# The head of a two-block decoder program: input in two transfers, identity and columns on the weights' queue, the root table loaded first, squares in one pass a row

## The reference, cut to what matters

```
def rmsnorm(x, g):                       # x: 256 x 1024
    y = x * rsqrt(mean(x * x, axis=-1) + EPS)
    return y * g

for i in range(2):                       # first block, two layers
    h = rmsnorm(x, norm1_g[i])
    z = h @ w_in[i] + b_in[i]            # q, k, v, gates ... of two mixers
    ...                                  # mixers, merge, feed-forward, gate
x = rmsnorm(x, final_g)
...                                      # second block, on x
```

## Time and profile before

| | |
|---|---|
| median of three runs | 3247.7 us |
| the profiled execution, its own time | 3248.43 us |
| its span, first to last instruction | 3246.6 us |
| around the span | 1.8 us |
| PE busy | 3170.3 us, 98% |
| DVE, ACT, POOL busy | 65%, 46%, 15% |
| mean granted clock of TensorE | 0.991 |

### The profile page before, as it was taken

The page is one execution under the profiler, slowest core; times in us unless marked ns, Lnnn a source line. Parts: engine busy times, 40 slices in busy tenths (PEclk is TensorE's granted clock), DMA queues, the critical chain, the costliest instruction groups (busy, mean ns, idle before and its releaser), DMA issues.

```text
span 3246.6 us, 49505 instructions
## 1 busy us (share of the span) xinstructions
PE 3170.3 (98%) x20652; PEld 2800.4 (86%) x20652; DVE 2109.0 (65%) x3115; ACT 1499.2 (46%) x1717; POOL 494.2 (15%) x278
## 2 busy tenths in 40 slices
PE   8999999999999999989999999999999999999998
PEld 8797889797978897878999989888769999999887
DVE  6775665577766656685967755555677867655555
ACT  6444454573444545612544444444344454444443
POOL 0000000000000000010766600000003766200000
PEclk9999999999999999999999999999999999999999
DMA  6454645444546554303454475555424544665553
GB/s 228 153 190 167 220 179 186 168 157 168 187 162 219 182 195 171 144 28 112 177 183 153 142 255 201 195 195 194 169 91 156 182 163 150 220 220 193 192 192 125
DMA packets 87656, 565.12 MB, mean 174 GB/s; under 512 B 10192, under 2 KB 10208, under 8 KB 23568
## 3 DMA queue, kind: packets, MB, share of 16 engines
q1 hardware_dynamic: 80496, 534.81, 45.9%
q0 software_dynamic: 6944, 27.21, 2.5%
HBM read 552.54 MB, written 9.44 MB: 173 GB/s over the span
## 4 chain that ended last, share of the span: by engine, by line
PE 53%; DVE 5%; ACT 1%; issue 1%; DVEq 0%; ACTq 0%
PE bank L2099 22%; PE bank L2127 7%; PE bank L2131 7%; PE bank L2126 7%; PE bank L2080 4%; ACT w_hi L2257 1%; PE bank L1797 0%; PE bank L1792 0%; PE bank L1793 0%; PE bank L2064 0%; DVE w_lo L2534 0%; DVE ymix L2755 0%; PE bank L1827 0%; PE bank L1828 0%; PE bank L1831 0%
## 5 line engine op out<-in xcount | busy, mean ns | idle before, releaser
L2257 ACT ACTIVATE w_hi<-raw 128x2048 fp32r<-128x2048 f32 x291 | 558.0, 1918 | 717.0 <-PE bank L2131 377.0
L2534 DVE TENSOR_TENSOR w_lo<-raw,w_hi 128x2048 fp32r<-128x2048 f32 x222 | 510.1, 2298 | 540.7 <-ACT w_hi L2257 539.9
L1055 DVE TENSOR_TENSOR w_lo<-raw,w_hi 128x2048 fp32r<-128x2048 f32 x200 | 458.1, 2292 | 319.3 <-ACT w_hi L816 317.5
L816 ACT ACTIVATE w_hi<-raw 128x2048 fp32r<-128x2048 f32 x201 | 384.9, 1917 | 443.7 <-PE bank L546 239.5
L2099 PE MATMUL bank<-act_hi,w_hi 128*128 128x256 f32 x2048 | 486.6, 281 | 0.0
L2099 PE MATMUL bank<-act_lo,w_hi 128*128 128x256 f32 x2048 | 482.1, 279 | 0.0
L2127 PE MATMUL bank<-w_hi,c_lo 128*128 128x512 f32 x1024 | 398.7, 389 | 0.0
L2126 PE MATMUL bank<-w_hi,c_hi 128*128 128x512 f32 x1024 | 398.7, 389 | 0.0
L2099 PEld LDWEIGHTS bank<-act_hi,w_hi 128*128 128x128 f32 x2048 | 385.5, 188 | 0.2
L2099 PEld LDWEIGHTS bank<-act_lo,w_hi 128*128 128x128 f32 x2048 | 385.4, 188 | 0.0
L1694 POOL TENSOR_TENSOR w_lo<-raw,w_hi 128x2048 fp32r<-128x2048 f32 x70 | 322.9, 4618 | 329.0 <-ACT w_hi L2257 171.4
(11 more groups left out here) (544 smaller groups left out, 5184.4 us busy)
## 6 DMA issues: line engine op xcount, KB each, us to landing
raw<-weights SPq DMA_DIRECT2D x492, 1024.0 KB, 4.8
row<-rows POOLq DMA_DIRECT2D x48, 256.0 KB, 4.3
spill<-staged SPq DMA_DIRECT2D x32, 256.0 KB, 3.1
hid<-spill SPq DMA_DIRECT2D x32, 256.0 KB, 4.8
y<-w_pe POOLq DMA_DIRECT2D x2, 1024.0 KB, 5.1
ln_row_mix<-ln_rows POOLq DMA_DIRECT2D x4, 512.0 KB, 4.9
hid<-keys POOLq DMA_DIRECT2D x2, 1024.0 KB, 6.3
ln_row_ffn<-ln_rows POOLq DMA_DIRECT2D x4, 512.0 KB, 7.7
```

The lines of the kernel that those rows point to most:

```text
L816: nc.scalar.activation(w_hi[:, k % SPLIT, :], raw[:, k % RAW, :], ACT.Copy).then_inc(hi_ready, 1)
L1055: nc.vector.tensor_tensor(w_lo[:, k % SPLIT, :], raw[:, k % RAW, :], w_hi[:, k % SPLIT, :].bitcast(F32), ALU.subtract).then_inc(lo_ready, 1)
L2257: A.activation(hi_of(k), raw[:, k % RAW, :], ACT.Copy).then_inc(hi_ready, 1)
L2534: V.tensor_tensor(lo_of(k), raw[:, k % RAW, :], hi_of(k).bitcast(F32), ALU.subtract).then_inc(lo_ready, 1)
```

## The change

x comes in two transfers, one a token half, each with a semaphore of its own; the identity goes between them and the columns behind them, both on SP's queue and both ahead of the weights. POOL's queue starts with the gate bias. A new `first_mean_square` loads the table of the root before it waits for x, and then makes for each half one pass of squares over all 1024 columns and the root. `gw_hi` on ACT goes behind the eight `act_hi`, `gw_lo` on DVE behind the eight `act_lo`, in both layers.

```
-    x_loaded = sem("x_loaded")
+    x_loaded = [sem(f"x_loaded{t}") for t in range(TT)]
+    col_first = sem("col_first")
...
-            sp.dma_start(x[:, :, :], x_in).then_inc(x_loaded, 16)
+            sp.dma_start(x[:, 0, :], x_in[:, 0, :]).then_inc(x_loaded[0], 16)
+            sp.dma_start(ident, identity).then_inc(ident_loaded, 16)
+            sp.dma_start(x[:, 1, :], x_in[:, 1, :]).then_inc(x_loaded[1], 16)
+            sp.dma_start(col[:, :], cols[0]).then_inc(col_first, 16)
...
-            pool.dma_start(ident, identity).then_inc(ident_loaded, 16)
...
-                pool.dma_start(col[:, :], cols[layer]).then_inc(col_loaded, 16)
+                    pool.dma_start(col[:, :], cols[layer]).then_inc(col_loaded, 16)
...
+            def first_mean_square():
+
+                act.wait_ge(eps_ready, 1)
+                do(nc.scalar.activation(spare[:, :], eps, ACT.Sqrt))
+                for t in range(TT):
+                    act.wait_ge(x_loaded[t], 16)
+                    do(nc.scalar.activation(junk[:, :], x[:, t, :], ACT.Square, accum_out=ssq[:, t:t + 1]))
+                    do(nc.scalar.activation(rstd[:, t:t + 1], ssq[:, t:t + 1], ACT.Sqrt, bias=eps, scale=1.0 / D), std_ready)
...
-                    if i or layer == 0:
+                    if i:
                         mean_square(3 * layer + i)
-                    if i == 0 and layer == 0:
+                    elif layer == 0:
+                        first_mean_square()
                         split_hi(0, 0, free=False)
                     if i == 0:
-                        act.wait_ge(col_loaded, layer * 32 + 32)
-                        do(nc.scalar.activation(gw_hi ..., ACT.Copy), gw_split)
+                        act.wait_ge(col_first, 16)
+                        if layer:
+                            act.wait_ge(col_loaded, layer * 32 + 16)
...                                      # the eight act_hi
+                    if i == 0:
+                        do(nc.scalar.activation(gw_hi ..., ACT.Copy), gw_split)
...                                      # on DVE: waits for the columns, the eight act_lo, then gw_lo
```

More of the change, by code:

```diff
@@ L820, in front_squares @@
             def front_squares(n):
[L822 to L826, removed]
+                act.wait_ge(front_added, n)
                 for t in range(TT):
@@ L831, in rest_squares @@
             def rest_squares(n, t):
-                if n:
-                    act.wait_ge(half_added, TT * (n - 1) + t + 1)
+                act.wait_ge(half_added, TT * (n - 1) + t + 1)
                 do(nc.scalar.activation(junk[:, CW:D], x[:, t, CW:D], ACT.Square, accum_out=ssq[:, t:t + 1]))
@@ L859, in norm @@
                 def norm(i):
-                    if i or layer == 0:
+                    if i:
                         mean_square(3 * layer + i)
-                    if i == 0 and layer == 0:
+                    elif layer == 0:
+                        first_mean_square()
                         split_hi(0, 0, free=False)
                     if i == 0:
-                        act.wait_ge(col_loaded, layer * 32 + 32)
-                        do(nc.scalar.activation(gw_hi[:, :, :].rearrange("p k n -> p (k n)"), col[:, COL["gatew"]:COL["gatew"] + 64], ACT.Copy), gw_split)
+                        act.wait_ge(col_first, 16)
+                        if layer:
+                            act.wait_ge(col_loaded, layer * 32 + 16)
                     g0 = COL[f"norm{i + 1}"]
@@ L875, in norm @@
                             do(ins, n_hi)
+                    if i == 0:
+                        do(nc.scalar.activation(gw_hi[:, :, :].rearrange("p k n -> p (k n)"), col[:, COL["gatew"]:COL["gatew"] + 64], ACT.Copy), gw_split)
                 def mixed(first, k0, banks=range(KD // 2)):
@@ L1090, in norm @@
                         split_lo(base, 0)
[L1091 to L1095, removed]
+                        dve.wait_ge(col_first, 16)
+                        dve.wait_ge(col_loaded, layer * 32 + 16)
                     g0 = COL[f"norm{i + 1}"]
@@ L1101, in norm @@
                                                   op0=ALU.mult, op1=ALU.subtract), n_lo)
+                    if i == 0:
+                        dve.wait_ge(gw_split, 1 + layer * A_LAYER["gw_split"])
+                        V.tensor_tensor(gw_lo[:, :, :].rearrange("p k n -> p (k n)"), col[:, COL["gatew"]:COL["gatew"] + 64],
+                                        gw_hi[:, :, :].rearrange("p k n -> p (k n)").bitcast(F32), ALU.subtract).then_inc(gw_split, 1)
                 def mixed(first, k0, banks=range(KD // 2)):
```

## The result

| | before | after |
|---|---|---|
| median, 20 runs each (lowest to highest) | 3246.86 us (3240.89 to 3252.16) | 3252.1 us (3244.38 to 3259.97) |
| profiled execution | 3248.43 us | 3253.41 us |
| its span | 3246.6 us | 3251.6 us |
| mean granted clock | 0.991 | 0.991 |

The ratio is 1.0015, 95% interval 1.0009 to 1.0022: 5.2 us slower, with an interval of 2.9 to 7.1. The forecast was 3250.0, 2.3 us slower than the 3247.7 of the three runs shown, and 3252.1 lies just inside its range of 3242.0 to 3252.5. It is slower, as forecast, by twice the forecast step.

The account below looks back on a forecast made before the run. PE bounds the kernel, busy 3170 of 3246.6 us, so only its idle head could be given back. Later first matmul 0.5, cold clock 1.6 and layer 1 0.2 make 2.3 us slower: 3250.0 us, range 3242.0 to 3252.5.

Parts of the forecast that it names:

- Part 1: Head: x's halves land at 4.1 and 5.9, transposes begin at 6.8; this alone gains 5.8 us.
- Part 2: Weight tile 0, sharing the engines with POOL's earlier constants, lands at 13.6 (bounds 8.6 to 14.2), and ACT waits for it.
- Part 3: PE's first real matmul at 16.4, 0.5 us later than before; bounds 4.5 gained to 1.1 lost.
- Part 4: PE idles between transposes and first matmuls, which then run on the low clock: 1.6 us lost, bounds 0 to 3.4.
- The gate product: Rival: the shifted head shortens, lengthens or moves the slow-clock stretch at the gate matmuls; 1.7 us either way, no separate chance.
- Part 5: Layer 1: gw_hi ahead of a copy without slack costs PE some 0.2 us, bounds 0 to 0.25.
- the class: Whole kernel's step against 6.5 us, what the measurement can tell: same 0.91, faster 0.06, slower 0.03.
- half of the gain: Rival: tile 0 lands as before, first matmul 2.4 us earlier, PE gap of 3 us; 3245.5 us, chance 0.22.

Follow-up runs that it names:

- e7: The changed kernel with 5 and 6 unused matmuls behind the halves' transposes, keeping PE busy; median 3264.94 us against 3255.24 for the kernel before.
- e8: The changed kernel with identity and columns back at the front of POOL's queue, x still in halves; 3256.03 us against 3255.24 for the kernel before.
- e2: The kernel before with the new queues alone, ACT waiting for both halves of x and keeping its old list; 3253.42 us against 3247.95.
- e3: The changed kernel with POOL's constants and rows held until weight tile 0 lands, gate bias still first; 3247.78 us against 3247.95 for the kernel before.
- e5: The changed kernel with POOL's gate bias, constants and rows all held until weight tile 0 lands; 3256.2 us against 3255.24 for the kernel before.
- e6: The kernel before with ACT's new order, and POOL's bias, constants and rows held until weight tile 0 lands; 3253.78 us against 3255.24.

## Why the prediction was right, and where its size was off

**Part 1, x by halves.** The first half was forecast to land at 4.1, with bounds of 4.1 and 5.7, and landed at 4.75; first transpose 7.5 against 6.8. The second half was forecast at 5.9 and landed at 11.7. This step failed. The bias was expected on the engines from 5.3, on the end of x or on tile 0; its packets begin at 3.83 in the trace, in the middle of x. The step counted bytes in SP's queue (64 KB of identity ahead), gave x none of the bias's stall and none of the sharing with the constants ("perhaps on the end of x's second half" stood in part 2 with no price), and took the identity at the rate of large packets. The runs give rough prices: with POOL silent 7.7, with the bias alone 9.7, with the constants alone 11.0. It also took the transfer as one; twelve sixteenths of it were there by 7.4, and the last four made the rest. It cost little in the end, because tile 0 is later still: with x's second half at 11.7 alone, ACT would have reached the tile at 13.3, and that is where its wait begins.

**Part 2, the weights.** The mechanism was right: POOL's constants, issued 1.1 us earlier, meet tile 0, and ACT waits for it. The size was not: 13.6 forecast, bounds 8.6 and 14.2, measured 17.2, and 17.0 with the queues alone. The term that was mis-sized is the data still ahead of the tile. From 7 us on, the sum had 0.12 MB of columns and 1.05 of weights; but in 7 to 10 us SP's queue moved 0.17 MB in 101 small packets, a third of the 0.18 MB/us taken from the earlier trace rows. Those rows show turn-taking between 8 KB packets and the constants'; with packets of 0.9 to 4 KB at the front of SP's queue the turns are the same and the bytes fewer. From 12 us, with weights at its front, and from 13.3 the rows' 4 KB packets instead of the constants' beside it, SP's queue had 68% of the engines and 1.39 MB in 5 us. The last 2 us, from twelve sixteenths of the tile at 15.3 to the whole at 17.2, are again a few stragglers, which the sum did not have.

The page "DMA: Bandwidth & Descriptors" of the Trainium skill, section "Queues, rings and completion order", which the prediction cited for turns packet by packet, is borne out again by the trace after, 93 packets to 101, where the packets of the two queues differ much more in size than in the earlier trace rows. What it implies for small packets the prediction did not draw.

**Part 3, the first real matmul.** From the tile's landing the chain was right: 17.2 + 1.9 + 0.1 + 0.8 is 20.0, measured 19.76. Against the forecast of 0.5 later it is 3.9 later, all of the difference from part 2.

**Part 4, the clock.** Forecast 1.6, measured 1.9: the second tile begins 5.8 behind where the first real matmul was 3.9 behind. e7 confirms the cause, with 2.39 and 1.98 us for the first two groups of sixteen.

The prediction weighed the page "TensorE: Matmul & The Clock Gate" of the Trainium skill, section "Part 4: PE-mode transpose", by which the full clock does not engage for transposes. e8 speaks against it again: after 3 us of transposes alone the first record of the full level is at 10.49, and e2's first sixteen matmuls behind transposes took 2.08.

**The gate product**, a rival worth 1.7 either way, came on top. In the old trace the low level held from 30.1 to 40.3, in the new one from 38.2 to 45.0, 3.4 us less, which at half speed gives 1.7 back; the step is 5.8 at the second tile and 4.2 at the 192nd matmul, 1.6 back. The kernel before, behind the earlier trace rows:
```profile
35.00:40.00 5.00, 5.00 (x25) 5.00 (x25) 4.35 (x7) 3.28 (x5) 0.00 (x0) 0.50 0.08 13
40.00:45.00 5.00, 5.00 (x45) 5.00 (x45) 1.26 (x4) 1.54 (x1) 0.00 (x0) 0.97 0.49 200
```
The 48 small matmuls began at 27.52 before and ran on the low level after the first 2.5 us; in the changed kernel they began at 33.32 and were nearly through when the level fell. Windows of the changed kernel (columns as above):
```profile
35.00:40.00 5.00, 5.00 (x39) 5.00 (x39) 0.84 (x3) 3.90 (x9) 0.00 (x0) 0.82 0.31 131
40.00:45.00 5.00, 5.00 (x25) 5.00 (x25) 4.77 (x8) 2.86 (x4) 0.00 (x0) 0.50 0.35 123
```

**Part 5, layer 1.** Forecast 0.2, measured 0.22 and, alone, 0.17.

**The sum.** 3.9 + 1.9 - 1.6 + 0.2 = 4.4, against 5.0 between the two profiled executions and 5.2 between the medians; the remaining 0.6 to 0.8 is within what executions drift behind the head. The forecast's 2.3 was 0.5 + 1.6 + 0.2. The sign and the class were right, and so were the terms of the clock and of layer 1. Tile 0's landing was 3.6 us off, and the gate product hid nearly half of that error. The first matmul, 3.9 later, lies beyond the upper bound of its own term (1.1), and the median, 0.4 us inside the range, stayed there because the wide bound on the clock left room and the gate product gave 1.6 back. That is partly luck. Small slips in the working change nothing: 16.5 less 2.4 is 14.1 and not 14.2, and half of the gain would be 3245.3 and not 3245.5.

## What to carry to other kernels

When a transfer is moved to another queue, count its packets there and not only its bytes, and ask which packets of the other queue take turns with it: small rows at the front of a queue give their turns away to large constants (0.12 MB against 0.38 in the same 2 us). Look at when the last sixteenth of a transfer lands, and not only at rates. Holding what is not needed early (here a bias and constants) behind the first tile brought the first real matmul forward in each kernel that did it, though no total is shown to have fallen by it. And read a gain at the head at the n-th instruction behind it, since the end of a 3 ms program drifts by more than the gain.

## What the runs showed of the hardware that was not expected

- A 32-byte row broadcast to 128 partitions, 4 KB in all, brings both queues down to 0.04 to 0.07 MB in the microsecond from 4.5 us in four kernels (0.32 and 0.38 without it), and alone goes with a second half of x 2.0 us later (e3 against e5, one execution each).
- The identity takes 128 packets on SP's queue and the columns 128; SP's queue brings 0.70 MB in 2 us with packets of 8 KB, 0.55 with x in 4 KB packets, 0.50 with the identity among these (e6, e8, e5).
- The landing of a 512 KB transfer in such traffic is set by its last sixteenths: x's second half came at 11.7, 9.9 and 13.1 in three executions with the same queues, and its eighth step of 16 at 7.2, 7.3 and 7.7.
- One chip of three ran the kernel before 7 to 9 us slower (3255.24 against 3247.95 and 3246.06, medians of 33 to 35 runs).
